# Two-layer encoder with expert routing: weight pieces loaded in the output projection, statistics applied after it is projected, a later chunk split, other counts of unread products

## The reference

```python
h = rms_norm(x, norm_mix[i])          # x * rsqrt(mean(x*x) + eps) * gain
x = x + attention(h, ...)             # layer 0 dilated windows, layer 1 banded with grouped keys
h = rms_norm(x, norm_ffn[i])
x = x + expert_choice_ffn(h, ...)     # 16 experts, each takes its top tokens; SwiGLU
```

## Time and profile before

| | us |
|---|---|
| three runs, median (lowest to highest) | 1817.66 (1816.83 to 1822.87) |
| the profiled execution, its time | 1821.69 |
| its span, first to last instruction | 1819.9 |
| PE busy | 1759.2 (97%) |
| VectorE busy | 1323.9 (73%) |
| ACT busy | 1132.7 (62%) |
| POOL busy | 233.3 (13%) |
| mean granted clock of TensorE | 0.988 of full speed |
| read from DRAM | 454.30 MB, mean 267 GB/s with the writes |

### The profile page before, as it was taken

How to read it: one execution, slowest core, us unless ns; L and a number is a source line. 1 busy time by engine, 2 the same in 40 slices (tenths; PEclk the granted TensorE clock), 3 DMA queues, 4 the chain that set the end, 5 groups by cost and what they waited for, 6 DMA issues and landing times.

```text
span 1819.9 us, 24456 instructions
## 1 busy us (share of the span) xinstructions
PE 1759.2 (97%) x10258; PEld 1386.3 (76%) x10258; DVE 1323.9 (73%) x1001; ACT 1132.7 (62%) x1186; POOL 233.3 (13%) x118
## 2 busy tenths in 40 slices
PE   8999999989999999999999999998999999999997
PEld 7988889967776776776779987996677767676765
DVE  4634455588888888888855556557888888888885
ACT  4343443357777777777744556335777777777774
POOL 0100000000010010011011100000112211211311
PEclk9999988999999999999999999999999999999999
DMA  4311113399999999999965012328999999999994
GB/s 162 96 51 56 39 58 109 140 338 395 389 379 382 391 387 374 395 389 371 397 214 123 21 33 59 107 93 330 395 396 391 377 391 393 376 386 391 381 388 140
DMA packets 156145, 486.04 MB, mean 267 GB/s; under 512 B 12503, under 2 KB 46423, under 8 KB 155991
## 3 DMA queue, kind: packets, MB, share of 16 engines
q1 hardware_dynamic: 148612, 459.30, 67.1%
q0 software_dynamic: 7424, 25.17, 5.9%
HBM read 454.30 MB, written 30.13 MB: 266 GB/s over the span
## 4 chain that ended last, share of the span: by engine, by line
PE 89%; ACT 4%; DVE 3%; DMA 2%; issue 1%; POOL 0%; SPq 0%; POOLq 0%; DVEq 0%; ACTq 0%
PE ps L1915 19%; PE ps L1917 19%; PE ps L1916 18%; PE ps L1609 5%; PE ps L1610 4%; PE ps L1611 4%; PE ps L1689 3%; PE ps L1545 2%; PE ps L1801 2%; PE ps L1802 2%; PE ps L1803 2%; PE ps L1661 2%; PE ps L1886 1%; PE ps L1678 1%; PE ps L1827 1%
## 5 line engine op out<-in xcount | busy, mean ns | idle before, releaser
L1358 DVE TENSOR_TENSOR w_lo<-ring,w_hi 128x2048 fp32r<-128x2048 f32 x384 | 876.3, 2290 | 150.7 <-ACT w_hi L1050 150.7
L1050 ACT ACTIVATE w_hi<-ring 128x2048 fp32r<-128x2048 f32 x384 | 736.2, 1918 | 285.2 <-PE ps L1917 264.7
L1915 PE MATMUL ps<-w_hi,xe_hi 128*96 128x512 f32 x1016 | 404.0, 398 | 4.2 <-DVE xe_lo L1492 4.2
L1917 PE MATMUL ps<-w_hi,xe_lo 128*96 128x512 f32 x1016 | 400.2, 394 | 0.0
L1916 PE MATMUL ps<-w_lo,xe_hi 128*96 128x512 f32 x1016 | 398.4, 392 | 0.0
L1915 PEld LDWEIGHTS ps<-w_hi,xe_hi 128*96 128x96 f32 x1016 | 164.1, 161 | 74.0 <-DVE xe_lo L1492 10.1
L1917 PEld LDWEIGHTS ps<-w_hi,xe_lo 128*96 128x96 f32 x1016 | 164.1, 161 | 71.6 <-issue 0.5
L1916 PEld LDWEIGHTS ps<-w_lo,xe_hi 128*96 128x96 f32 x1016 | 164.6, 162 | 65.0
L1915 PE MATMUL ps<-w_hi,hid_hi 128*96 128x512 f32 x512 | 201.6, 394 | 0.0
L1917 PE MATMUL ps<-w_hi,hid_lo 128*96 128x512 f32 x512 | 201.1, 393 | 0.0
L1916 PE MATMUL ps<-w_lo,hid_hi 128*96 128x512 f32 x512 | 200.3, 391 | 0.0
(11 more groups left out here) (209 smaller groups left out, 2245.2 us busy)
## 6 DMA issues: line engine op xcount, KB each, us to landing
ring<-in_moe_w_gate SPq DMA_DIRECT2D x128, 1024.0 KB, 7.6
ring<-in_moe_w_up SPq DMA_DIRECT2D x128, 1024.0 KB, 9.1
ring<-in_moe_w_down SPq DMA_DIRECT2D x128, 1024.0 KB, 9.5
wbuf<-in_a_w_in SPq DMA_DIRECT2D x8, 1024.0 KB, 5.5
ffn_rows<-hrow SPq DMA_DIRECT2D x12, 512.0 KB, 3.0
wbuf<-in_b_w_in SPq DMA_DIRECT2D x5, 1024.0 KB, 8.2
unit_rows<-row SPq DMA_DIRECT2D x36, 132.0 KB, 1.8
bias<-bias_rows SPq DMA_DIRECT2D x4, 768.0 KB, 10.4
```

What stands on the lines that cost most here:

```text
L1050: nc.scalar.activation(w_hi[:, n % SPLIT], ring[:, n % RAW], ACT.Copy).then_inc(hi_split, 1)
L1358: nc.vector.tensor_tensor(w_lo[:, n % SPLIT], ring[:, n % RAW], w_hi[:, n % SPLIT].bitcast(F32), ALU.subtract).then_inc(lo_split, 1)
L1915: nc.tensor.matmul(out, hi[:, k, :], w_hi[:, n % SPLIT, i, cols], start=(k == 0), stop=False)
L1917: ins = nc.tensor.matmul(out, lo[:, k, :], w_hi[:, n % SPLIT, i, cols], start=False, stop=(k == KM - 1))
```

## The change

Four edits, which reach into SP, VectorE, ACT and PE:

1. SP waits for the split of the layer's last chunk and issues two pieces (`AHEAD` = 2) ahead of the first row store, two more after the last projection, and the last two of the ring behind the last row store, with no wait for the gather in front of the sixth.
2. The second chunk is split two tiles later, in both layers: ACT's high half behind tile 3's take, VectorE's low half behind the low half of the last tile.
3. In layer 1 VectorE multiplies x by the gain alone, and ACT applies the row's power when it takes a projected tile out of PSUM, for all five chunks of q, k and v. Squares, means and powers go on beside this. The unread products ahead of it go from 60 to 46.
4. In the last group of layer 0 the unread products per unit go from 1 to 7 in the first unit and to 3 in the others.

```diff
-RAW, SPLIT, FRONT = 6, 4, 3
+RAW, SPLIT, FRONT, AHEAD = 6, 4, 4, 2
...
+                first_piece = layer * LAYER_PIECES
+                sp.wait_ge(chunk_lo, END_CHUNK[layer])
+                for n in range(first_piece, first_piece + AHEAD):
+                    load_piece(n)
                 for i in range(NT - 1):
                     store_rows(i)
                     store_sums(i)
                 sp.wait_ge(out_done, NT * (layer + 1))
-                first_piece = layer * LAYER_PIECES
-                for n in range(first_piece, first_piece + FRONT):
+                for n in range(first_piece + AHEAD, first_piece + FRONT):
                     load_piece(n)
                 store_rows(NT - 1)
-                for n in range(first_piece + FRONT, first_piece + RAW - 1):
+                for n in range(first_piece + FRONT, first_piece + RAW):
                     load_piece(n)
                 sp.wait_ge(xg_in[0], 16 * (layer * NE // 2 + 1))
-                for n in range(first_piece + RAW - 1, first_piece + LAYER_PIECES):
+                for n in range(first_piece + RAW, first_piece + LAYER_PIECES):
...
                 def take_transposed(step, dst, then=None, ahead=None):
                     for t in range(NT):
                         n = step * NT + t
-                        if layer and t + 2 < NT:
-                            ahead(t + 2)
                         act.wait_ge(h_turned, n + 1)
...
+                        if layer and t + 1 < NT:
+                            ahead(t + 1)
...
                     dst = {"q": qraw, "k": kraw, "v": v[:, g % 2]}[kind]
+                    if layer:
+                        act.wait_ge(rstd_ready, rstd_count(2 * layer, t))
+                        nc.scalar.activation(dst[:, t, :], ps[:, proj_bank(n), 0:GW], ACT.Copy,
+                                             scale=rstd[:, t:t + 1]).then_inc(qkv_taken, 1)
+                        return
...
                     sum_of_squares(2 * layer, 0)
-                    sum_of_squares(2 * layer, 1)
...
                     take_tile(FIRST_CHUNK[layer], t)
-                    if t == 1:
+                    if t == 3:
                         high_chunk(FIRST_CHUNK[layer] + 1)
...
                 def scale_row(s, part, t, dst):
 
+                    if layer:
+                        dve.wait_ge(x_in[t], 16 * (layer + 1))
+                        nc.vector.tensor_tensor(dst, x[:, t, :], gain[:], ALU.mult).then_inc(h_ready, 1)
+                        return
...
-                row_means(2 * layer, 0)
-                if layer:
-                    row_means(2 * layer, 1)
+                if layer == 0:
+                    row_means(2 * layer, 0)
...
-                    if 1 <= t < NT - 1:
+                    if layer == 0 and 1 <= t < NT - 1:
                         row_means(2 * layer, t + 1)
                     if t >= (1 if layer else 2):
                         low_rows(t - 1)
-                    if t == 3:
-                        low_chunk(FIRST_CHUNK[layer] + 1)
+                    if layer and t >= 1:
+                        row_means(2 * layer, t - 1)
                 low_rows(NT - 1)
+                low_chunk(FIRST_CHUNK[layer] + 1)
+                if layer:
+                    row_means(2 * layer, NT - 1)
...
-                    idle_products(60)
+                    idle_products(46)
...
                         if dense:
-                            idle_products(1)
+                            idle_products(7 if n == 2 * NT else 3)
```

## The result

The changed kernel takes 1802.43 us (median of four runs, 1802.26 to 1803.57) against 1817.24 for the kernel before (four runs, 1815.47 to 1822.87): a ratio of 0.9915, 95% interval 0.9893 to 0.9937. The forecast was 1801.5 in a range of 1795 to 1811. The profiled execution took 1803.57 us (span 1801.7, mean granted clock 0.995); that of before had 1819.9 and 0.988, so 18.2 us of span went.

A forecast was written before the change was run, and what follows sets the result against it. TensorE was taken to bound the kernel (89% of the chain), losing time where it waits or runs slowly. Terms summed to -17.2 us: 1804.5 from the profiled run, 1800.5 from the median; forecast 1801.5, range 1795 to 1811.

The forecast's parts named there:

- Split two tiles later, layer 0: Start of layer 0: PE's 2.06 us wait for tile 4 and a 1.7 us clock loss go, 0.8 us wait comes; -3.0.
- More products in the last group: Layer 0's last attention group: added unread products fill the 1.83 us wait and the clock holds; -5, other end +4.
- VectorE's mixed rows come some 2.8 us earlier: End of layer 0's last group: mixed rows ready at 279.2, so their transposes start at 279.3 instead of 284.63.
- Early pieces: Start of the experts: weight queue one piece further after the gather, waits and clock loss shrink; -4.1 layer 0, -1.5 layer 1.
- Layer 1's start: Layer 1: transposes start 2.6 us earlier after scaling by gain alone, and the moved split removes tile 4's wait; -3.9.
- The scale on 30 takes: Layer 1, ACT: per-row scale costs 0.09 us on each of 30 takes, 2.7 us in all; +0.3 on the path.
- the 1.0 us that I added: Final forecast set at 1801.5 instead of the median-based 1800.5, since some summed clock losses may be missing in other runs.
- the good ends named for the terms: Most favourable values of the separate gains; the range's lower end was put 6 us below the forecast for them.
- 1 (the clock falls anyway): Layer 0's last group: clock falls despite the added products, +4 instead of -5, 1810.5 us; chance 0.12.
- 2 (the gather behind the weights): Start of the experts: weight loads reach into the first gather, 5.1 us more per layer, about 1817 us; chance 0.05.
- 3 (the pieces bring nothing): Early weight pieces: later loads wait for freed slots, not transfers, so 5.6 us less gain, 1807 us; chance 0.10.
- 4 (the clock stays low into the projection): Layer 0's output projection: clock, down in the last group, stays low; slower, 1840 us at three tiles; chance 0.03.

The follow-up runs named there:

- u_split: The changed kernel with layer 0's second chunk split where it was before, layer 1 keeping the moved split; 1805.82 us.
- p_first: The changed kernel with seven unread products in the first unit of layer 0's last group but one in each other unit; 1805.3 us.
- p_others: The changed kernel with one unread product in the first unit of layer 0's last group and three in each other unit; 1804.82 us.
- u_wait: The changed kernel with two weight pieces still early, but the sixth again waiting for the first gather; 1808.21 us.
- u_ahead: The changed kernel without early weight pieces and with the sixth again behind the first gather, as before; 1808.72 us.
- l_late: The changed kernel with no early pieces, all six weight pieces behind the last projection and none waiting for the gather; 1808.53 us.
- g_fill: The changed kernel with ten more unread products ahead of the first expert's picks, in both layers; 1802.56 us.
- u_stats: The changed kernel with layer 1's statistics, plain takes and 60 unread products as before, the moved split kept; 1806.45 us.

## Why the prediction was right

The time came out 0.9 us above the forecast, and each of the five gains came where it was said to come, one of them by another cause than the prediction read. The terms one by one, against the columns:

- *Split two tiles later, layer 0.* Predicted -3.0, measured -2.97 from before to after and 2.7 by undoing it. The new wait was put at 0.8 us and is 0.80; since 0.8 was a choice between 0 and 1.91, that close a hit is luck. That the clock's 0.79 goes with the wait is shown by u_split, where both return.
- *More products in the last group.* Predicted -5, measured -4.1 (4.0 by undoing). Here the prediction has its two faults. The cause was wrong: I took the 1.83 us wait for what lowers the clock; p_first and p_others show that the products in the later units hold it. (The row that I gave only as support, layer 1's units with three products each at 1.00, was the better guide.) And the size was off, at the step where VectorE's mixed rows come some 2.8 us earlier: counted from the first products with v, they came 1.55 us earlier. The clock held and PE was at the last unread products even sooner than reckoned, 12.8 us behind those products instead of 13.8; but the transfer of the mixed rows, for which VectorE waits, started only 1.75 us earlier on SP's queue (268.32 - 257.01 = 11.31 us behind those products, 276.05 - 262.99 = 13.06 before). The store of the unit's rows ahead of it, for which SP waits, was issued 3.0 us earlier, about as reckoned (265.08 - 257.01 = 8.07 us behind the products, 274.04 - 262.99 = 11.05 before), but it landed 3.2 us behind its issue where it had taken 1.9. A load of 768 KB of `w_out` was issued 2.0 us ahead of it, before 3.2 us; that this load is the reason was not tested. SP's queue, and behind it the issue of that store (last figure: us to landing), before and then after:

```profile
276.05 0.37 SPq L648 DMA_DIRECT2D qraw<-unit_rows  x1
...
unit_rows<-row SPq DMA_DIRECT2D x1, 132.0 KB, 1.9
...
268.32 0.37 SPq L648 DMA_DIRECT2D qraw<-unit_rows  x1
...
unit_rows<-row SPq DMA_DIRECT2D x1, 132.0 KB, 3.2
```

  So PE stands 1.84 us at the mixed rows. VectorE's timeline of the changed kernel shows what it waits for itself:

```profile
271.87 0.17 DVE L1257 TENSOR_TENSOR mix_top<-qraw 128x4 f32<-128x4 f32 x1 [3.67 <-DMA qraw<-unit_rows]
...
273.53 0.96 DVE L1289 TENSOR_TENSOR v<-qraw,mix_c 128x768 f32<-128x768 f32 x1
```

- *Early pieces.* Predicted -4.1 and -1.5, measured -4.32 and -1.54. The reason given (the queue starts one piece further when the gather has landed) is confirmed by u_wait in layer 0. Of the 4.3 us, 2.8 are the wait and some 1.5 a clock loss behind it, which came in before and u_wait and not in u_ahead; the wait does not always bring it, and the prediction counted it, at 1.7 us, as if it did.
- *Layer 1's start.* Predicted -3.9 (2.6 statistics, 1.3 split), measured -3.83 (2.6 and 1.25). The transposes came 2.7 us earlier, as the landing of x plus one multiplication promised.
- *The scale on 30 takes.* Predicted +0.09 us each: 0.38 us has become 0.47. On the path I put 0.3; nothing shows there. Groups by line of the changed kernel, with and without the scale:

```profile
L840 ACT ACTIVATE kraw<-ps,rstd 128x256 f32<-128x256 f32 x6 | 2.9, 475 | 8.1 <-PE ps L1624 8.1
L843 ACT ACTIVATE kraw<-ps 128x256 f32<-128x256 f32 x18 | 6.9, 383 | 47.5 <-PE ps L1624 47.3
```

The edits together gave -2.97 - 4.10 - 4.32 - 3.83 - 1.54 = -16.8 us against the -17.2 predicted. The profiles differ by 18.2 because the changed kernel's first profile lacked the dip behind the table products (-3.0) and had one ahead of the experts (+1.5). The medians differ by 14.8 only: the profiled execution of before lies high among that kernel's runs, at 1821.69 us. I had seen that it lay 4.0 us above its median, and took the forecast from the median with a little added; that was the right choice. Which of its losses the other runs of before lacked stays open, since they left no trace.

That the forecast is off by only 0.9 us is in part luck. Undoing the parts one by one gives 2.7 + 4.0 + 2.8 + 1.6 + 2.6 + 1.25 = 15.0 us, near the 14.8 between the medians, each of them with the scatter named above. Set against a median, the sum of 17.2 was thus some 2 us too large, chiefly by the clock loss behind the experts' first wait and by the last group; the 1.0 us that I added made up for part of that. The range's lower end, 1795, is not borne out by its own working either: the good ends named for the terms add up to 2.7 us (0.8 + 0.3 + 0.3 + 1.0 + 0.3), not 6.

Of the rivals: 1 (the clock falls anyway) did not come, but p_first shows that it would have with the first unit's products alone. 2 (the gather behind the weights) did not come in the changed kernel, and did in l_late, at 0.9 to 2.1 us of PE's waiting per layer instead of 5.1. 3 (the pieces bring nothing) and 4 (the clock stays low into the projection) are out; the projection takes 86.9 to 87.0 us in every kernel.

## What to carry to other kernels

Cut the span at fixed instructions and compare stage by stage: where whole spans scatter by 3 us from clock dips, the experts' stages still gave a part's worth to 0.1 us and the last group to 0.6; the start of layer 0 scatters by 1.6 itself, which only further profiles of the same program could tell. Before loads are moved ahead of a small transfer that the critical engine waits for, reckon from the queue's own rows when the last of them will be through, and which store ahead of that transfer they delay; the same six loads made PE wait 2.1 us at the gather or not at all, by whether two of them left early. Where filler work holds a clock, test its places one at a time: the place with the longest wait need not be the one that matters.

## What the runs showed of the hardware

The clock fell in work without a wait: behind the four table products (33 rows by 12 columns of weights) it went to 0.50 in six of ten profiles of the same stretch, and in neither of the two with the products parted by a projection tile. It fell behind a wait of 1.2 us for a gather in g_fill's layer 0; in its layer 1, behind a like wait of 0.9 us, it kept 1.00, in layer 0's last group it kept 1.00 behind 1.84 us, and in u_ahead's experts behind 2.7 us. So in these traces the length of the wait just before does not tell by itself whether the clock will fall.

POOL's power operation on one column took 1.46 to 1.48 us in four of layer 1's six tiles in the changed kernel and 0.55 in the others, where u_stats has 1.55 once; PE did not wait for it. The first of the four begins at 942.37 us, while VectorE multiplies x by the gain (942.20 to 943.42). The gather's instruction on POOL showed the like: 2.65 us in l_late's layer 0, where it began during a subtraction of VectorE, and 1.15 us in all other profiles, where it began ahead of it.
